# Two transformer blocks on one core, last mixer: the additions that build the compression blocks move from GpSimd to the vector engine

## The reference, cut to what matters

```python
q, k_c, v_c, k_s, v_s, k_w, v_w, z, g_logit = jnp.split(h @ w_in, np.cumsum(sizes).tolist(), axis=-1)
...
n_cmp = (S - CMP_BLOCK) // CMP_STRIDE + 1          # 15
tok_idx = cmp_start[:, None] + jnp.arange(CMP_BLOCK)[None, :]
def compress(t, pe, w1, w2):
    blocks = t[:, tok_idx] + pe[:, None, :]
    flat = blocks.transpose(0, 1, 3, 2, 4).reshape(B, n_cmp, G, CMP_BLOCK * DK)
    return jax.nn.silu(flat @ w1) @ w2
k_cmp = compress(k_c, cmp_pe[0], cmp_w1[0], cmp_w2[0])
v_cmp = compress(v_c, cmp_pe[1], cmp_w1[1], cmp_w2[1])
```

## Time and profile before

| | |
|---|---|
| median of 3 runs | 925.53 us (925.20 to 926.27) |
| profiled execution | 925.01 us, its span 923.3 us |
| PE busy | 913.1 us, 99% of the span |
| DVE / ACT / POOL busy | 686.2 / 550.4 / 72.7 us |
| the mixer's first projection matmul | 761.3 us after the span's start |
| first attention scores | 810.1 us |

### The profile page before, as it was taken

The page is one execution under the profiler, slowest core; times in us unless marked ns, Lnnn a source line. Parts: engine busy times, 40 slices in busy tenths (PEclk is TensorE's granted clock), DMA queues, the critical chain, the costliest instruction groups (busy, mean ns, idle before and its releaser), DMA issues.

```text
span 923.3 us, 16713 instructions
## 1 busy us (share of the span) xinstructions
PE 913.1 (99%) x6101; PEld 809.7 (88%) x6101; DVE 686.2 (74%) x1270; ACT 550.4 (60%) x977; POOL 72.7 (8%) x96
## 2 busy tenths in 40 slices
PE   9999999999999999999999999999999999999997
PEld 8999888888888987888888888999899789999985
DVE  4978678767667788688675686999576768778875
ACT  5654465545455678566554545866577645477783
POOL 0000011111110000100000000000000005332200
PEclk9999999999999999999999999999999999999999
DMA  8665557776665332676666555444245565423312
GB/s 317 219 206 170 192 186 230 219 222 202 204 211 183 114 116 86 204 283 206 204 187 198 185 170 169 139 139 137 69 137 206 166 198 186 145 95 107 120 37 88
DMA packets 43757, 158.11 MB, mean 171 GB/s; under 512 B 5456, under 2 KB 6240, under 8 KB 42928
## 3 DMA queue, kind: packets, MB, share of 16 engines
q1 hardware_dynamic: 41520, 147.79, 49.7%
q0 software_dynamic: 1888, 8.77, 2.6%
q10 hardware_dynamic: 288, 0.72, 0.3%
HBM read 155.82 MB, written 1.05 MB: 170 GB/s over the span
## 4 chain that ended last, share of the span: by engine, by line
PE 91%; DVE 4%; ACT 3%; DMA 1%; issue 1%; SPq 0%; DVEq 0%; ACTq 0%
PE ps L782 16%; PE ps L560 8%; PE ps L561 8%; PE ps L562 8%; PE ps L780 8%; PE ps L615 8%; PE ps L619 8%; PE ps L617 8%; PE ps L777 2%; PE ps L1157 2%; DMA raw<-stream_dram 1%; PE ps L1106 1%; PE ps L1132 1%; PE ps L778 1%; DVE wl L1804 1%; PE ps L598 1%
## 5 line engine op out<-in xcount | busy, mean ns | idle before, releaser
L1804 DVE TENSOR_TENSOR wl<-raw,wh 128x1024 fp32r<-128x1024 f32 x270 | 333.3, 1240 | 102.0 <-ACT wh L1243 50.5
L1243 ACT ACTIVATE wh<-raw 128x1024 fp32r<-128x1024 f32 x174 | 182.1, 1058 | 108.0 <-DMA raw<-stream_dram 96.3
L782 PE MATMUL ps<-hxa,wh 128*128 128x512 f32 x616 | 219.4, 396 | 0.0
L560 PE MATMUL ps<-hxa,wh 128*128 128x256 f32 x672 | 196.4, 292 | 1.0 <-DVE wl L1804 0.5
L561 PE MATMUL ps<-hxa,wh 128*128 128x256 f32 x672 | 190.1, 283 | 0.0
L562 PE MATMUL ps<-hxa,wl 128*128 128x256 f32 x672 | 190.0, 283 | 0.0
L780 PE MATMUL ps<-hxa,wl 128*128 128x256 f32 x616 | 172.1, 279 | 0.0
L1411 ACT ACTIVATE wh<-raw 128x1024 fp32r<-128x1024 f32 x96 | 101.5, 1058 | 61.7 <-DMA raw<-stream_dram 22.7
L782 PEld LDWEIGHTS ps<-hxa,wh 128*128 128x128 f32 x616 | 115.8, 188 | 23.8
L560 PEld LDWEIGHTS ps<-hxa,wh 128*128 128x128 f32 x672 | 128.4, 191 | 7.9 <-issue 4.6
L561 PEld LDWEIGHTS ps<-hxa,wh 128*128 128x128 f32 x672 | 128.7, 191 | 0.2
(11 more groups left out here) (380 smaller groups left out, 1308.7 us busy)
## 6 DMA issues: line engine op xcount, KB each, us to landing
raw<-stream_dram SPq DMA_DIRECT2D x271, 512.0 KB, 4.2
biasm<-bias_dram POOLq DMA_DIRECT2D x12, 192.0 KB, 4.1
w<-w_dram POOLq DMA_DIRECT2D x1, 2048.0 KB, 8.9
mlw<-mlw_dram POOLq DMA_DIRECT2D x1, 1056.0 KB, 6.4
x<-x_dram SPq DMA_DIRECT2D x1, 1024.0 KB, 7.8
mem<-memT_dram SPq DMA_DIRECT2D x1, 1024.0 KB, 8.5
memx<-mem_dram SPq DMA_DIRECT2D x1, 1024.0 KB, 5.9
grow<-rows_dram POOLq DMA_DIRECT2D x2, 512.0 KB, 4.0
```

What stands on the lines that cost most here:

```text
L560: pe.matmul(o, wh[:, w_s, w_cols], act[hi], start=start, stop=False, skip_group_check=True)
L782: return pe.matmul(o, wh[:, s % RING, wc], hx[:, k, :, :], start=False, stop=(k == KC - 1), skip_group_check=True)
L1243: act.activation(wh[:, v % RING, :], raw[:, v % RAW, :], ACT.Copy).then_inc(wh_ready, 1)
L1804: dve.tensor_tensor(wl[:, s % RING, :], raw[:, s % RAW, :], wh[:, s % RING, :].bitcast(F32), ALU.subtract).then_inc(wl_ready, 1)
```

## The change

All 32 additions are now done by DVE: `late_blocks` becomes `blocks(j, th)`, called ahead of each of the eight takes j = 2 to 9 with four additions each: kc0 ahead of vc0 and vc1, kc1 ahead of ks0 and ks1, vc0 ahead of kw0 and kw1, vc1 ahead of q0 and (before `rotate()`) vs. Each of the four parts counts up `blk_ready`. POOL's part is gone.

```diff
-            def late_blocks(th):
+            def blocks(j, th):
 
+                kv, kc = j // 2, j % 2
                 if th == 0:
-                    dve.wait_ge(proj_taken, PN[("vc", 1)].n + 1)
+                    dve.wait_ge(proj_taken, PN[N_PRE[j]].n + 1)
-                view = vraw[:, 1, :].rearrange("p (b a q) -> p a b q", a=8, q=2)
+                view = (kraw, vraw)[kv][:, kc, :].rearrange("p (b a q) -> p a b q", a=8, q=2)
...
+                if 2 <= j <= 9:
+                    blocks((j - 2) // 2, j % 2)
                 if j == 9:
                     rotate()
-                if j in (5, 6):
-                    late_blocks(j - 5)
...
-            for j in range(3):
-                pool.wait_ge(proj_taken, PN[N_PRE[j]].n + 1)
-                blocks(j // 2, j % 2).then_inc(blk_ready, 1)
```

More of the change, by code:

```diff
@@ L2445, in rotate @@
                 dve.tensor_tensor(nqr[:, 0, :], nqr[:, 0, :], nqr[:, 7, :], ALU.add).then_inc(q_roped, 1)
-            def late_blocks(th):
+            def blocks(j, th):
+                kv, kc = j // 2, j % 2
                 if th == 0:
-                    dve.wait_ge(proj_taken, PN[("vc", 1)].n + 1)
-                view = vraw[:, 1, :].rearrange("p (b a q) -> p a b q", a=8, q=2)
+                    dve.wait_ge(proj_taken, PN[N_PRE[j]].n + 1)
+                view = (kraw, vraw)[kv][:, kc, :].rearrange("p (b a q) -> p a b q", a=8, q=2)
                 for par in range(2):
                     rows = slice(HD * par, HD * par + HD)
-                    pos = col("pe", 32, 32, rows).rearrange("p (a q) -> p a q", q=2)
+                    pos = col("pe", 32 * kv, 32, rows).rearrange("p (a q) -> p a q", q=2)
                     for q in range(2):
                         e = dve.tensor_tensor(
-                            blk[HD * q:HD * q + HD, 1, 8 * th:8 * th + 8, 2 + par, :], view[rows, :, th:th + NCMP, q],
+                            blk[HD * q:HD * q + HD, kv, 8 * th:8 * th + 8, 2 * kc + par, :],
+                            view[rows, :, th:th + NCMP, q],
                             pos[:, 8 * th:8 * th + 8, q].unsqueeze(2).to_broadcast([HD, 8, NCMP]), ALU.add)
@@ L2723, in _ @@
             pool.dma_start(grow2[:], rows_d[1]).then_inc(grow2_landed, 16)
[L2725 to L2737, removed]
             pool.wait_ge(lo_ready, 64)
```

## The result

The changed kernel took 928.30 us (median of 8 runs), the kernel before 925.67 us beside it (8 runs); the ratio is 1.0030, 95% interval 1.0021 to 1.0039. I had predicted 925.8 us and no measurable difference. The kernel became 0.3% slower. One of the eight runs of the changed kernel lasted 2306.88 us; the ratio leaves it out, and nothing here explains it. The median of eight counts it; the median of the other seven is 928.09 us.

What follows compares the result with a forecast made beforehand. PE, busy for 99% of the span, was taken as the bound; gate logits 0.3 us late turn 925.01 us into 925.3, and 0.52 for the median gives 925.8 us. Range for 8 in 10: 925.0 to 927.3.

Steps and rivals of the forecast that it cites:

- What bounds the kernel: PE, busy for 99% of the span; with no gap there to close, faster DVE or POOL work wins nothing.
- The removal on POOL: Taking POOL's 24 additions away gives 0 by itself; DVE gets 0.22 to 0.25 us back on most subtractions.
- What an addition costs on DVE alone: One addition on DVE without POOL beside it was put at 0.283 us, four at 1.19 us.
- both bounds: Limits for one DVE addition: 0.23 to 0.24 us without the 0.04, 0.44 to 0.49 with no waiting inside the rows.
- strided reads: Rival: DVE's reads 64 bytes apart take a second step, an addition 0.41 us, the kernel 928.8 us or 929.6; chance 12%.
- three remainders: Three DVE additions beside POOL, 0.45 to 0.54 us, each left about 0.27 us once the waiting was taken out.
- the 0.04 us: Estimated time from a DVE instruction's start until it begins to read.
- Where the take lands: DVE's take of kw1 ends at 788.20, before 787.62; PE's gate logits, waiting for it, start 0.3 us late.
- The loads: Copies of u10 and u11 stay hidden by 0.7 to 0.8 us; SP's last fetch ends some 0.5 us later.
- The last additions: DVE's last additions, 1.2 us, fit into its wait before the rotation and end near 796.6; PE wants them at 797.0.
- The sum: 925.01 us for the profiled execution becomes 925.3; with 0.52 for the median, 925.8 us.

Runs made afterwards that it cites:

- the version with short additions: The changed kernel with all 32 additions reading adjacent elements (values not the reference's): 925.39 us, ratio 0.9993.
- one wait moved: The changed kernel with the gate logits on PE waiting for the take of ks1 in place of kw1: 925.90 us, ratio 1.0008.
- second profile: Profile from running the changed kernel again with nothing edited: 929.28 us (5 runs), ratio 1.0039.

## Why the prediction was wrong, point by point

**What bounds the kernel: right.** PE had no gap to close, and no version came out below the kernel before by more than the scatter.

**The removal on POOL: right.** Every subtraction fell to 1.21 to 1.23 us, and no time was won by it.

**What an addition costs on DVE alone: the step that failed.** I put 0.283 us; it is 0.357. I had both bounds, 0.23 and 0.44 to 0.49, and the rival with the reason, strided reads; I gave it 12% because three remainders agreed. They could agree because a row beside GpSimd does not show the price. (Without the 0.04 us the three remainders are 0.23, 0.23 and 0.22, not 0.23 to 0.24; nothing hangs on it.) The rival's own size was too large: it charged 1.05 ns for each element, and the runs show 0.65. It was to decide from 0.35 us on, and the true value fell just past that.

**Where the take lands: right in form.** With 0.357 in the same sum kw1's take ends at 788.20 + 24 x 0.074 = 789.98, and in an execution that is 0.13 us later at the subtraction of 772 at 790.11; it ended at 790.17. The gate logits would start 2.1 us late by my working; counted from the first projection matmul they started 2.05 us later than before. (The list of waits says 1.88, since it counts from the end of the matmul before.) In the version with short additions they were 0.16 us late where I had forecast 0.3.

**The loads: right for u10 and u11, too small behind them.** In the changed kernel ACT copied u10 at 780.40 and u11 at 783.80, and DVE waited for neither ahead of kw1's take. But I let SP's last fetch end some 0.5 us later than before; it ended at 797.33 in place of 795.35, 2.0 us later. The take of ks0, which the first fetch waits for, was itself later by the longer additions. That is not all: in the version with short additions it ended at 796.73, 0.9 us later than before once the 0.5 us of a later execution are taken off. The rotation began at 798.51, not near 797.

**The last additions: partly wrong.** I let them end at 796.6, in time for the compression. They ended at 798.03, which only the gap on PE covered; with that gap gone, the wait of 1.0 us came to light (one wait moved). The four are only 0.3 us longer together than I had reckoned. The rest is the subtraction ahead of them: it waited 1.13 us for ACT's copy of u14, whose load SP issued at 790.62, behind the late fetches, in place of 788.64. In the version with short additions they ended at 797.12 in an execution that is 0.5 us later, which is my 796.6.

**The sum: one term was missing.** A gap on PE cost only the time by which the work behind it started late, in my working. From the first projection matmul to the first scores the kernel before takes 48.82 us, the changed one 50.88 in its first profile, 2.06 more, which is that cost alone. In the second profile it takes 52.52, 3.70 more: the fall of the clock adds 1.6 us, and for that I had no term. In all fourteen profiles what lies behind the first scores lasts 113.1 to 113.4 us, and the first projection matmul comes between 761.1 and 764.2; so the scatter between profiles that neither gap nor clock explains lies ahead of the stretch. With 2.06 the first median would be 927.7; it was 928.3, or 928.1 without the long run. The clock is part of that difference; how large a part was not separated from the scatter. Why the clock falls in some executions after 1.9 us, in the one profiled after 4.8, and not in those profiled after 0.6, 1.0, 1.4 and 1.7, was not settled.

## What to carry to other kernels

The duration of an instruction that another engine's instruction held up need not be its duration alone plus a wait; a price of its form need not show in that row, so take it from a run or keep the upper bound. Where work is moved onto an engine that stands close to a deadline, look for the one wait on the bounding engine that names a late result: here a wait for a later take than the data needed turned 1.8 us of extra work into a gap. Read a tile in the order in which it is stored, or pay for the turning once at the write.

## What the hardware showed that I had not expected

- A float32 addition of VectorE whose first input steps by 16 bytes or more costs 0.63 to 0.85 ns more for each element than with steps of 4 or 8 bytes (0.278 against 0.354 to 0.380 us for 120 elements, 0.397 against 0.562 for 240). Writing 256 elements 64 bytes apart, from PSUM, cost 0.62 us in place of 0.42.
- Beside GpSimd's additions, an addition of VectorE lasted 0.44 to 0.54 us with reads 4 bytes or 64 bytes apart.
- After a gap of 1.9 us on TensorE the granted clock fell to 0.50 for at least 3.2 us, beginning 1.4 us after the work had resumed, in one of two profiled executions; after 4.8 us it was 0.50 from the first matmul, for 5.1 us. At 0.50 the float32 matmuls with 256 columns started 0.21 us apart in place of 0.12.
